# Two transformer blocks in one launch: heads turned inside the last value product, a stepwise second product of the feed-forward, state copies and low halves reordered

## The reference, cut to what matters

```
# first block, layer 0: differential attention, then a squared-relu feed-forward
qkv = rms_norm(h) @ w_qkv                       # 1024 x 3072: q, k, v
q, k = rope(rms_norm(q)) * 64**-0.5, rope(rms_norm(k))     # 8 heads, 2 parts of 64 each
p = softmax(q k^T)  per head and part
attn = p[:, 0] - lam * p[:, 1];  o = attn @ v   # lam = exp(lv0.lv1) - exp(lv2.lv3) + lam_init
h = h + rms_norm(o) * (1 - lam_init) @ w_o
h = h + square(relu(rms_norm(h) @ w_up)) @ w_down          # 1024 -> 4096 -> 1024
# layer 1: a state-space layer (two scans over 512 tokens), gelu, val * sigmoid(gate)
# @ w_glu; then the same feed-forward.  Second block (its output is also returned):
# adaptive layer norm, convolution beside latent attention, merge, and at the end
u = dwconv(norm(h) @ w_up2)                     # 1024 -> 2 x 2816, kernel of 3 tokens
y = (silu(g) * val) @ w_down2                   # 2816 -> 1024
out = layer_norm(alpha * x + g2 * y)
```

## Time and profile before

| what | value |
|---|---|
| median of 3 runs | 1922.88 us (1919.81 to 1924.55) |
| profiled execution | 1924.76 us |
| its span, first to last instruction | 1923.0 us |
| around the span | 1.76 us |
| PE busy | 1820.7 us (95%) |
| DVE busy | 1295.9 us (67%) |
| ACT busy | 785.3 us (41%) |
| mean granted clock of TensorE | 0.980 |

### The profile page before, as it was taken

How to read it: one execution, slowest core, us unless ns; L and a number is a source line. 1 busy time by engine, 2 the same in 40 slices (tenths; PEclk the granted TensorE clock), 3 DMA queues, 4 the chain that set the end, 5 groups by cost and what they waited for, 6 DMA issues and landing times.

```text
span 1923.0 us, 25971 instructions
## 1 busy us (share of the span) xinstructions
PE 1820.7 (95%) x9518; PEld 1477.7 (77%) x9518; DVE 1295.9 (67%) x2443; ACT 785.3 (41%) x1276; POOL 39.2 (2%) x35
## 2 busy tenths in 40 slices
PE   7998999999999992999999999999999999999898
PEld 6785578888888862788888788789787778888786
DVE  4766866866886659536655787359887766676365
ACT  5226864432343363334421342345676353333111
POOL 0000000000000000000000000000132000000000
PEclk9999999999999996999999999999999999999999
DMA  6330002355555479333444666123101223223422
GB/s 205 100 99 23 1 16 97 127 153 162 161 156 156 144 251 146 132 101 129 153 143 146 211 226 211 66 97 101 43 13 45 66 77 100 96 94 102 163 90 75
DMA packets 99930, 225.02 MB, mean 117 GB/s; under 512 B 19296, under 2 KB 48608, under 8 KB 99824
## 3 DMA queue, kind: packets, MB, share of 16 engines
q1 hardware_dynamic: 53520, 166.81, 28.2%
q10 hardware_dynamic: 46304, 56.77, 9.6%
HBM read 202.68 MB, written 20.87 MB: 116 GB/s over the span
## 4 chain that ended last, share of the span: by engine, by line
PE 83%; DVE 11%; ACT 3%; issue 2%; DMA 1%; ACTq 1%; DVEq 0%; SPq 0%
PE PS L434 25%; PE PS L436 24%; PE PS L435 24%; PE PS L978 1%; DVE ST L2044 1%; DVE Sst L2051 1%; DVE Sst L2048 1%; PE PS L627 1%; DVE mx L1846 1%; PE PS L609 1%; DVE WL L1575 1%; PE PS L962 1%; DVE Ca L2139 1%; PE PS L542 1%; PE PS L970 1%
## 5 line engine op out<-in xcount | busy, mean ns | idle before, releaser
L1575 DVE TENSOR_TENSOR WL<-raw,WH 128x1024 fp32r<-128x1024 f32 x228 | 277.3, 1222 | 306.5 <-ACT WH L1062 295.3
L1062 ACT CAST WH<-raw 128x1024 fp32r<-128x1024 f32 x228 | 237.3, 1046 | 519.0 <-PE PS L436 449.6
L434 PE MATMUL PS<-XH,WH 128*128 128x512 f32 x928 | 365.9, 394 | 5.3 <-DVE XL L1609 5.1
L436 PE MATMUL PS<-XH,WL 128*128 128x512 f32 x928 | 362.3, 390 | 0.0
L435 PE MATMUL PS<-XL,WH 128*128 128x512 f32 x928 | 362.1, 390 | 0.0
L434 PE MATMUL PS<-WH,AH 128*128 128x512 f32 x688 | 270.5, 393 | 5.4 <-DVE AL L2342 5.4
L436 PE MATMUL PS<-WH,AL 128*128 128x512 f32 x688 | 268.6, 390 | 0.0
L435 PE MATMUL PS<-WL,AH 128*128 128x512 f32 x688 | 268.5, 390 | 0.0
L434 PE MATMUL PS<-WH,XH 128*128 128x512 f32 (+2 forms) x512 | 198.4, 388 | 16.1 <-DVE XL L1645 10.5
L434 PEld LDWEIGHTS PS<-XH,WH 128*128 128x128 f32 x928 | 174.9, 188 | 43.9 <-DVE XL L1609 6.0
L436 PEld LDWEIGHTS PS<-XH,WL 128*128 128x128 f32 x928 | 174.8, 188 | 36.6
(11 more groups left out here) (357 smaller groups left out, 2483.4 us busy)
## 6 DMA issues: line engine op xcount, KB each, us to landing
raw<-units_dram SPq DMA_DIRECT2D x272, 512.0 KB, 3.3
...
```

The source lines that it names most:

```text
L434: pe.matmul(o, lh, rh, start=start, stop=False)
L436: return pe.matmul(o, ll, rh, start=False, stop=stop)
L1062: nc.scalar.copy(WH[:, (u + n) % SLOTS], raw[:, s]).then_inc(hi_done, 1)
L1575: v.tensor_tensor(WL[:, s], raw[:, (u + n) % 2], WH[:, s].bitcast(F32), ALU.subtract).then_inc(unit_ready, 1)
```

## The change

Edits in six places:

- Start: silu(c) and the exponentials of `lam` move on ACT from before unit 6 to behind the first half of the value tiles; DVE's wait for `lam_exp` and its three small instructions move behind the rotation of k.
- Last value product: chunk 5 is cut into its four units. Behind each of the first three, two heads are turned (`head_turned`: q and k of a head, eight transposes) through banks 4 to 7. Heads 6 and 7 are turned behind the second score product, and their copies stand inside the first rounds of ACT and DVE.
- The second half of the value tiles is copied by ACT (tiles 0, 2) and DVE (tiles 1, 3), each tile with a signal of its own.
- The low and high halves of the first four output-projection units are interleaved with the head copies; the fourth `lo` moves behind the whole attention.
- Scan: `TURN_AT` is (14, 17), so `gelu_lo(2)`, `gelu_lo(3)` stand after step 17; `gelu(4)` on ACT stands behind all the state copies.
- Second product of the last feed-forward: its first chunk goes to banks 4 to 7 and waits for `u2_lo` unit by unit; the wait for `u2_conv` stands before the second chunk, which takes banks 0 to 3; `merge` reads the banks the other way round.

```diff
--- before.py
+++ after.py
@@ -48,7 +48,7 @@
 LAG = 20
-PRE, WARM, TURN_AT = 48, 13, 14
+PRE, WARM, TURN_AT = 48, 13, (14, 17)
 ROW_LOADS = (4, 7, 10)
@@ -564,24 +564,30 @@
 
-                for c in range(6):
+                def head_turned(hh):
+
+                    for which in range(2):
+                        if hh >= 2:
+                            pe.wait_ge(qt_copied[which], hh - 1)
+                        for t in range(NT):
+                            m = pe.transpose(psum(4 + 2 * (hh % 2) + which)[:, t * P:(t + 1) * P], (U, Kt)[which][:, t, hh * P:(hh + 1) * P], ident[:, :])
+                        m.then_inc(qt_turned, 1)
+
+                for c in range(5):
                     if c >= 2:
...
                 pe.wait_ge(qk_ev, 4 * NT)
-                pe.wait_ge(v_ev, 2)
-                pe.wait_ge(x_in, 16 * 9)
-                for which in range(2):
-                    src = (U, Kt)[which]
-                    for hh in range(HEADS):
-                        n = which * HEADS + hh
-                        if n >= 4:
-                            pe.wait_ge(qt_copied[(n - 4) // HEADS], (n - 4) % HEADS + 1)
-                        for t in range(NT):
-                            m = pe.transpose(psum(n % 4)[:, t * P:(t + 1) * P], src[:, t, hh * P:(hh + 1) * P], ident[:, :])
-                        m.then_inc(qt_turned, 1)
-                pe.wait_ge(qt_copied[0], HEADS)
-                pe.wait_ge(qt_copied[1], HEADS)
+                for i in range(4):
+                    token_chunk(UNITS["qkv"] + 20, 0, XH, XL, first=2 * i, last=2 * i + 2)
+                    if i == 0:
+                        pe.wait_ge(v_ev, 1)
+                        pe.wait_ge(x_in, 16 * 9)
+                    if i < 3:
+                        head_turned(2 * i)
+                        head_turned(2 * i + 1)
+                for copied in qt_copied:
+                    pe.wait_ge(copied, HEADS - 2)
                 NI = HEADS * NT
@@ -604,15 +610,23 @@
                             pe.wait_ge(at_e, 2 * (n - 1))
+                        else:
+                            pe.wait_ge(v_ev, n + 2)
+                            pe.wait_ge(qk_ev, 4 * NT + n + 1)
                         for c in range(2):
...
                         m.then_inc(at_s, 1)
+                    if n == 1:
+                        for hh in (6, 7):
+                            head_turned(hh)
                     if 2 <= n <= NI + 1:
...
                             pe.wait_ge(at_c, i - 1)
+                        else:
+                            pe.wait_ge(qt_copied[i], 7)
                         for kt in range(NT):
@@ -623,6 +637,8 @@
                             pe.wait_ge(at_o, i - 1)
+                        else:
+                            pe.wait_ge(qt_copied[i], 8)
                         for kt in range(NT):
@@ -1019,11 +1035,10 @@
                     up2(i)
-                pe.wait_ge(u2_lo, FT2)
+                token_chunk(UNITS["down2"], 4, AH2, AL2, kt=FT2, ready=lambda k: pe.wait_ge(u2_lo, k))
                 pe.wait_ge(u2_conv, 2 * FT2)
-                for c in range(2):
-                    token_chunk(UNITS["down2"] + 11 * c, 4 * c, AH2, AL2, kt=FT2, last=14 if c else None)
-                chunk_by_tile(UNITS["down2"] + 11, 14, 4, AH2, AL2, FT2)
+                token_chunk(UNITS["down2"] + 11, 0, AH2, AL2, kt=FT2, last=14)
+                chunk_by_tile(UNITS["down2"] + 11, 14, 0, AH2, AL2, FT2)
 
@@ -1136,10 +1151,6 @@
 
-                a.wait_ge(consts_in, 16 * 11)
-                nc.scalar.activation(c_act[:, :, :], c_col[:, :, :], ACT.Silu)
-                a.wait_ge(lam_sum, 1)
-                nc.scalar.activation(lams[:, 2:4], lams[:, 0:2], ACT.Exp).then_inc(lam_exp, 1)
                 hi(SLOTS + 2, 2)
@@ -1151,16 +1162,27 @@
                 a.wait_ge(norm_inv, 1)
-                for c in range(4, 6):
-                    a.wait_ge(unit_used, UNITS["qkv"] + 4 * c + 4)
-                    for t in range(NT):
-                        m = nc.scalar.activation(Vt[:, t, 512 * (c - 4):512 * (c - 3)], psum(4 * (1 - c % 2) + t), ACT.Copy, scale=ss[:, t:t + 1])
-                    m.then_inc(v_ev, 1)
-                    if c == 4:
-                        hi(UNITS["wo"], 4)
-                for hh in range(HEADS):
-                    a.wait_ge(qt_turned, hh + 1)
-                    nc.scalar.copy(QT[:, hh, :], psum(hh % 4)).then_inc(qt_copied[0], 1)
+                def query_copied(hh):
+
+                    a.wait_ge(qt_turned, 2 * hh + 1)
+                    nc.scalar.copy(QT[:, hh, :], psum(4 + 2 * (hh % 2))).then_inc(qt_copied[0], 1)
+
+                a.wait_ge(unit_used, UNITS["qkv"] + 20)
+                for t in range(NT):
+                    m = nc.scalar.activation(Vt[:, t, 0:512], psum(4 + t), ACT.Copy, scale=ss[:, t:t + 1])
+                m.then_inc(v_ev, 1)
+                a.wait_ge(consts_in, 16 * 11)
+                nc.scalar.activation(c_act[:, :, :], c_col[:, :, :], ACT.Silu)
+                a.wait_ge(lam_sum, 1)
+                nc.scalar.activation(lams[:, 2:4], lams[:, 0:2], ACT.Exp).then_inc(lam_exp, 1)
+                for i in range(3):
+                    query_copied(2 * i)
+                    query_copied(2 * i + 1)
+                    hi(UNITS["wo"] + i)
+                a.wait_ge(unit_used, UNITS["qkv"] + 24)
+                for t in (0, 2):
+                    nc.scalar.activation(Vt[:, t, 512:D], psum(t), ACT.Copy, scale=ss[:, t:t + 1]).then_inc(v_ev, 1)
+                hi(UNITS["wo"] + 3)
                 NI = HEADS * NT
@@ -1184,6 +1206,8 @@
                                                  bias=nb[:, n, c:c + 1], accum_out=es[:, n, c:c + 1]).then_inc(at_e, 1)
+                        if n < 2:
+                            query_copied(6 + n)
                     if n >= 2:
@@ -1352,8 +1376,10 @@
                         states(n, 0 if q else PRE)
-                        if n == 4 * q + 1:
-                            gelu(n - 1)
+                        if n == 1:
+                            gelu(0)
+                    if q:
+                        gelu(4)
                     gelu(4 * q + 1)
@@ -1661,11 +1687,6 @@
 
-                v.wait_ge(lam_exp, 1)
-                step(v.tensor_scalar(lams[:, 3:4], lams[:, 3:4], LAM_INIT, None, ALU.subtract))
-                step(v.tensor_tensor(lams[:, 0:1], lams[:, 3:4], lams[:, 2:3], ALU.subtract))
-                step(v.tensor_scalar(subln[:, 1:2], subln[:, 0:1], 1.0 - LAM_INIT, None, ALU.mult))
-
                 par = lambda i: pt[:, i, :]
@@ -1825,10 +1846,23 @@
                         lo(UNITS["qkv"] + 4 * c + 8 + t)
-                lo(UNITS["wo"], 4)
-                for hh in range(HEADS):
-                    v.wait_ge(qt_turned, HEADS + hh + 1)
-                    v.tensor_copy(KT[:, hh, :], psum(hh % 4)).then_inc(qt_copied[1], 1)
+                v.wait_ge(lam_exp, 1)
+                step(v.tensor_scalar(lams[:, 3:4], lams[:, 3:4], LAM_INIT, None, ALU.subtract))
+                step(v.tensor_tensor(lams[:, 0:1], lams[:, 3:4], lams[:, 2:3], ALU.subtract))
+                step(v.tensor_scalar(subln[:, 1:2], subln[:, 0:1], 1.0 - LAM_INIT, None, ALU.mult))
+
+                def key_copied(hh):
+
+                    v.wait_ge(qt_turned, 2 * hh + 2)
+                    v.tensor_copy(KT[:, hh, :], psum(5 + 2 * (hh % 2))).then_inc(qt_copied[1], 1)
+
+                for i in range(3):
+                    key_copied(2 * i)
+                    key_copied(2 * i + 1)
+                    lo(UNITS["wo"] + i)
+                v.wait_ge(unit_used, UNITS["qkv"] + 24)
+                for t in (1, 3):
+                    v.tensor_scalar(Vt[:, t, 512:D], psum(t), ss[:, t:t + 1], None, ALU.mult).then_inc(qk_ev, 1)
                 NI = HEADS * NT
@@ -1845,6 +1879,8 @@
                         max_done = order.n
+                        if n == 1:
+                            key_copied(6)
                     if 1 <= n <= NI:
@@ -1867,6 +1903,8 @@
                                                op0=ALU.mult, op1=ALU.add).then_inc(at_a, 1)
+                        if n == 1:
+                            key_copied(7)
                     if n >= NI:
@@ -1881,6 +1919,7 @@
                 entry_lo(t_o, o_gain, 0, range(4, KD))
+                lo(UNITS["wo"] + 3)
                 rates()
@@ -2071,9 +2110,10 @@
                     scan([(i - LAG, 8, 4), (i - LAG, 12, 4)])
-                    if i == NCH - 1 + TURN_AT:
-                        gelu_lo(0)
-                        gelu_lo(1)
+                    for half in range(2):
+                        if i == NCH - 1 + TURN_AT[half]:
+                            gelu_lo(2 * half)
+                            gelu_lo(2 * half + 1)
 
@@ -2086,8 +2126,6 @@
 
-                gelu_lo(2)
-                gelu_lo(3)
                 for n in range(4, 8):
@@ -2293,7 +2331,7 @@
                                 v.wait_ge(unit_used, u_last[1])
```

(2 more changed lines are left out.)

## The result

The changed kernel takes 1903.05 us (median of 4 runs, 1901.98 to 1904.99) against 1923.72 us for the kernel before on the same chip: a ratio of 0.9891, 95% interval 0.9874 to 0.9908, that is 21.0 us less (17.7 to 24.2). The forecast was 1901, range 1896 to 1908. The profiled execution took 1903.85 us with a span of 1902.1, 20.9 less than the span before; the prediction's sum was 22.0.

The account below looks back on a forecast made before the run. PE, busy 95% of the span, was taken as the bound, leaving its idle holes and the slow clock behind them. 4.5 + 7.1 + 3.0 + 7.4 = 22.0 us off 1924.76, 1.9 less against the median: 1901, range 1896 to 1908.

Parts of the forecast that it names:

- Start: Before the first casts: both table loads go, 2.93 us, and slow clock behind PE's wait, 1.55; 4.5 us gained.
- Value product: Last value product to first scores: first score gains 7.9 us, 0.8 given back by the fourth exponential; 7.1 gained.
- Scan: State-space layer: PE's wait in the gated product shrinks from 1.80 to 0.4 us, 1.4, clock 1.6; 3.0 gained.
- Second product: Last feed-forward: PE's wait for all low tiles goes, 5.3 us, and slow clock behind it, 2.1; 7.4 gained.
- Third load: Table load before the root of the first q tiles goes too, but DVE's sums hid it: nothing gained.
- fifth gelu: State-space layer: `gelu(4)` behind the state copies changes no wait of PE: nothing.
- row loads: Last product: the fifth unit's low half waits for them, with 4.2 us of cover: nothing lost.
- The fourth low half: Output projection's fourth unit, made later with 2.2 us of cover: nothing; without cover up to 1.2 us.
- The first: Rival: the holes close but the clock still falls behind three of them; 16.8 us gained, 1906; chance 0.13.
- The second: Rival: the front of the attention binds on copies, 3.5 us gained there in place of 7.1; 1904.5; chance 0.10.
- The third: Rival: nothing measurable, as later stages wait for something that does not move; 1920; chance 0.03.
- The fourth: Rival: transposes between units let the clock fall in the last value product; 13 us slower, 1936; chance 0.04.

Follow-up runs that it names:

- a_ref: The changed kernel itself, measured again: ratio 0.9893 to the kernel before, median 1903.6 us.
- s_start: Kernel before, with only the table loads moved from the start into the value product: ratio 0.9981, 3.7 us less.
- s_heads: Kernel before, with only the heads turned inside the last value product and the attention, copy and low-half edits belonging to it: ratio 0.9961, 7.5 us less.
- a_wait: Changed kernel, but the last feed-forward's second product waits for all 22 low halves first, banks kept: ratio 0.9940 to the kernel before.
- a_gelu: Changed kernel, with the fifth gelu again between the state copies: ratio 0.9892 to the kernel before.
- a_ca: Changed kernel, with the first six `CA` loads held back until all `Tm` loads have landed: ratio 0.9895 to the kernel before.
- a_lo3: Changed kernel, with the output projection's fourth low half back ahead of the attention: ratio 0.9904 to the kernel before, median 1904.8 us.
- a_noscan: Changed kernel, with the third and fourth gelu tiles' low halves again behind the scan: ratio 0.9895 to the kernel before, median 1903.1 us.
- s_down: Kernel before, with only the last feed-forward's second product taking its low halves one by one, on the other banks: ratio 0.9962, 7.3 us less.
- s_scan: Kernel before, with only the third and fourth gelu tiles' low halves made at the 17th step of the scan's tail: ratio 0.9996, 0.8 us less.

## Why the prediction was right, step by step

- **Start, 4.5.** The 2.93 us of loads are gone in every trace. The 1.55 of clock was right for the execution that was profiled, and is not the rule: two of the four executions with the old start kept the full clock, behind a hole that was 1 us shorter (2.01 and 2.17 instead of 3.17 and 3.16), since the slow matmuls at the kernel's start were more and PE came to it later. The Trainium skill says that the count of slow matmuls at a kernel's start differs from run to run of one kernel ("TensorE: Matmul & The Clock Gate", section "What's actually happening"). The two traces of the changed kernel agree: 10 of its first 24 matmuls are at the slow spacing in one, 13 in a_ref. Measured 3.7 (1.7 to 5.6).
- **Value product, 7.1.** The first score was to come 6.15 us behind the old end of the product, and came there: 148.28 - 4.5 + 6.15 = 149.9 against 149.81. (The lead at the chunk's start was 4.8, 0.7 of it from the fifth unit's earlier transfer, and the rest took 6.3.) Three groups of 16 transposes, priced at 1.8 us each, put the next unit back by 1.70, 1.77 and 1.80. The piece that came out otherwise is the 0.8 given back by the fourth round's exponential: from the first round to the fourth it takes 7.09 us, 7.26 before. The copies are not free, though. In the kernel before the clock fell in the third round (0.66 from 167 to 172 us), behind a wait of 2.3 us of PE for the first exponentials; that wait is 0.4 now, since PE turns heads 6 and 7 in it. In s_start, with the old order and no such fall, the same stretch takes 6.56 (timeline of ACT, first and fourth round, and a window):

```profile
160.47 0.78 ACT L1185 ACTIVATE E<-PS,nb,qsc 128x512 f32<-128x512 f32 x1 [7.28 <-DVE nb L1854]
...
167.03 0.78 ACT L1185 ACTIVATE E<-PS,nb,qsc 128x512 f32<-128x512 f32 x1
```

```profile
163.00:167.00 4.00, 2.79 (x15) 1.20 (x13) 3.96 (x10) 3.12 (x9) 0.00 (x0) 1.00 0.00 0
```

  So at the same clock the copies cost 0.5, near the 0.8 of the forecast, and the baseline of 7.26 held 0.7 of slow clock, which went too. Another 0.7 to 0.8 is lost ahead of the scan in the changed kernel's first trace. There the first sixteen matmuls of the state blocks ran at full clock, PE then waited 2.12 us for a state copy that DVE had not made, and the clock fell behind that wait; the blocks take 18.3 us up to the scan. It is chance and not the change: so it went in s_heads, a_wait, a_gelu and a_ca too, but in a_ref, the same kernel, the sixteen were slow, no such wait came, and the blocks take 17.5, as before (timelines of PE, after and a_ref):

```profile
689.95 0.63 PE L776 MATMUL PS<-ident,S 128*128 128x128 f32 x4 [2.12 <-DVE Sst L2071]
690.51 1.67 PE L763 MATMUL PS<-WI,UG 128*64 128x256 f32 x8
```

```profile
683.87 3.68 PE L763 MATMUL PS<-WI,UG 128*64 128x256 f32 x16
```

- **Scan, 3.0.** Mis-sized, the one term that was clearly too large. The mechanism is right: the wait goes where it existed, and where PE comes earliest it is 0.35 us (a_wait, a_lo3), as worked out (0.4). Alone the part measured 0.8 (-1.3 to 2.9), undone 0.0 (-1.6 to 1.6). The step read both its pieces, the wait and the clock of 0.52, from one execution and took them for fixed. Neither is. The wait depends on when PE comes to the gated product. Where it starts 0.06 us behind DVE's second low half, the hole is 1.80 (before) or 1.76 (a_noscan); where it starts 0.77, 1.35 and 2.16 behind it, the hole is 1.07 (s_heads), 0.50 (s_down) and none (s_start). Late lags make PE late in s_start and s_heads; in s_down, with the earliest lags, it was a slow clock in the outputs behind a wait of 4.54 us for the state copies. And the clock kept 1.00 behind three of the four holes. In the profile the 3.7 us won between the gated product and the fifth output stand against 3.0 lost at late lags, a loss that the forecast did not hold and that is chance.
- **Second product, 7.4.** 7.65 in each trace: wait 5.3 and clock 2.3. Behind this hole the clock fell in every trace that has it, five in all (before, s_start, s_heads, s_scan, a_wait; the first matmul takes 0.79 or 0.80 in each). The fifth unit's low half waited for the row loads until 1790.01, as named, with PE needing it at 1773.46 + 4 x 5.44 = 1795.2.
- **Nothing for the rest.** Third load, fifth gelu, row loads: seen as nothing. The fourth low half: its new place costs nothing, and its old one would have cost 1.2 in the trace of a_lo3.
- **The sum.** 22.0 against the profiled execution, 20.9 measured; its parts by the table are 11.8 up to the first exponential, -0.7 to the scan, 0.9 to the fifth output, 0.6 to the last activation, 7.6 to the end and 0.7 from the earlier transfer of the fifth unit. The runs' own 20.6 and 21.0 agree. The scan term's shortfall of 2.1 was half made up by small things, and the 0.6 and 0.7 among them are chance. Chance took part on the other side too: in the late lags (3.0 lost) and in the state blocks (0.7 lost). That 20.9 came so near to 22.0 is thus in part luck of one trace; the medians' 21.0 and 20.6 are not of one trace, and the scan term and the clock's 1.55 in the start term hold in some executions only.
- **Rivals.** The first (clock falls all the same) is false at all three places. The second (attention bound by copies) has 0.5 us of its 3.6 in it. The third (nothing measurable) is false. The fourth (transposes lower the clock) is false: 1.00 from 120 to 150 with 48 transposes in it. The Trainium skill ("TensorE: Matmul & The Clock Gate", section "Part 4: PE-mode transpose") has transposes not count as work for the clock gate; that the clock stayed up here, with 1.7 us of them at a time between products of 5.4 us, neither confirms nor refutes that, and the rise at 155 in the kernel before stays the place where trace and page differ.
